# Gated delta: the 16x16 diagonal blocks inverted on VectorE by forward substitution, two doubling levels kept on TensorE

## The reference

```python
lower = jnp.where(strict, jnp.einsum('bhncd,bhned->bhnce', kb, k) * decay, 0.0)
tri = lower + jnp.eye(GDN_CHUNK, dtype=jnp.float32)
rhs = jnp.concatenate([v * beta[..., None], kb * jnp.exp(gc)[..., None]], axis=-1)
sol = lax.linalg.triangular_solve(tri, rhs, left_side=True, lower=True, unit_diagonal=True)
...
def step(state, xs):
    u_i, w_i, qh_i, kt_i, intra_i, gl_i = xs
    v_new = u_i - jnp.einsum('bhcd,bhde->bhce', w_i, state)
    o = (jnp.einsum('bhcd,bhde->bhce', qh_i, state)
         + jnp.einsum('bhce,bhef->bhcf', intra_i, v_new))
    state = (state * jnp.exp(gl_i)[..., None, None]
             + jnp.einsum('bhcd,bhce->bhde', kt_i, v_new))
    return state, o
```

## Time and profile before

| | us |
|---|---|
| median of 3 runs (2565.07 to 2569.24) | 2565.99 |
| span of the profiled execution | 2562.7 |
| PE busy (share of the span) | 2382.4 (93%) |
| DVE busy | 1392.5 (54%) |
| GpSimd busy | 1326.4 (52%) |
| ACT busy | 595.4 (23%) |

### The profile page before, as it was taken

How to read it: one execution, slowest core, us unless ns; L and a number is a source line. 1 busy time by engine, 2 the same in 40 slices (tenths; PEclk the granted TensorE clock), 3 DMA queues, 4 the chain that set the end, 5 groups by cost and what they waited for, 6 DMA issues and landing times.

```text
span 2562.7 us, 38766 instructions
## 1 busy us (share of the span) xinstructions
PE 2382.4 (93%) x14272; PEld 1896.6 (74%) x14272; DVE 1392.5 (54%) x1992; ACT 595.4 (23%) x1162; POOL 1326.4 (52%) x1018
## 2 busy tenths in 40 slices
PE   0888999998999999999999999999999999999996
PEld 0666777786777777777876877778777777887885
DVE  8965654656555554575135265155656554234536
ACT  0221210222323332232023022022322323224001
POOL 6673457434444445556655644644444444454763
PEclk9998999999999999999999999999999999999998
DMA  9864347322122123454325533532122222222542
GB/s 364 291 229 161 116 161 254 125 85 65 59 67 65 61 67 115 148 192 164 95 73 202 173 109 106 187 115 75 59 67 62 63 67 67 66 80 69 181 140 90
DMA packets 94600, 316.14 MB, mean 123 GB/s; under 512 B 10918, under 2 KB 11174, under 8 KB 93382
## 3 DMA queue, kind: packets, MB, share of 16 engines
q1 hardware_dynamic: 86768, 295.51, 34.1%
q10 hardware_dynamic: 7644, 18.16, 2.0%
HBM read 303.92 MB, written 8.39 MB: 122 GB/s over the span
## 4 chain that ended last, share of the span: by engine, by line
PE 71%; DVE 15%; POOLq 3%; ACT 3%; issue 3%; DMA 2%; POOL 2%; DVEq 1%; ACTq 1%; SPq 0%
PE bank L644 14%; PE bank L646 13%; PE bank L645 13%; DVE arena L1693 11%; PE bank L1159 4%; PE bank L1161 4%; PE bank L1160 4%; DVE acc L1693 3%; PE bank L925 2%; PE bank L954 2%; POOLq L1635 1%; POOL w_lo L1633 1%; ACT arena L1189 1%; PE bank L608 1%; PE bank L946 1%
## 5 line engine op out<-in xcount | busy, mean ns | idle before, releaser
L1629 POOL CAST w_hi<-ring 128x1024 fp32r<-128x1024 f32 (+1 forms) x320 | 363.5, 1136 | 1105.7 <-PE bank L646 922.6
L1633 POOL TENSOR_TENSOR w_lo<-ring,w_hi 128x512 fp32r<-128x512 f32 (+1 forms) x632 | 881.5, 1415 | 48.5 <-issue 1.3
L644 PE MATMUL bank<-h_hi,w_hi 128*128 128x512 f32 x1952 | 827.9, 424 | 14.1 <-POOLq L1635 12.3
L646 PE MATMUL bank<-h_hi,w_lo 128*128 128x512 f32 x1952 | 768.7, 394 | 0.0
L645 PE MATMUL bank<-h_lo,w_hi 128*128 128x512 f32 x1952 | 767.6, 393 | 0.0
L644 PEld LDWEIGHTS bank<-h_hi,w_hi 128*128 128x128 f32 x1952 | 370.6, 190 | 101.1 <-issue 16.4
L646 PEld LDWEIGHTS bank<-h_hi,w_lo 128*128 128x128 f32 x1952 | 369.1, 189 | 83.0
L645 PEld LDWEIGHTS bank<-h_lo,w_hi 128*128 128x128 f32 x1952 | 371.2, 190 | 69.3 <-issue 7.2
L1189 ACT ACTIVATE arena<-bank 128x512 f32<-128x512 f32 (+5 forms) x372 | 173.8, 467 | 737.5 <-PE bank L646 216.6
L1693 DVE SCALAR_TENSOR_TENSOR acc<-yT,cact,acc 128x1024 f32<-128x1024 f32 (+1 forms) x144 | 209.6, 1456 | 37.9 <-DMA acc<-in_b_mod 14.9
L1159 PE MATMUL bank<-w_hi,h_hi 128*128 128x512 f32 x448 | 175.4, 392 | 1.1 <-issue 1.1
(11 more groups left out here) (226 smaller groups left out, 2911.7 us busy)
## 6 DMA issues: line engine op xcount, KB each, us to landing
ring<-in_stream SPq DMA_DIRECT2D x352, 512.0 KB, 3.6
yT<-in_stream SPq DMA_DIRECT2D x128, 512.0 KB, 4.5
yT<-in_mod SPq DMA_DIRECT2D x32, 1024.0 KB, 8.2
arena<-in_x ACTq DMA_DIRECT2D x4, 1024.0 KB, 10.3
x_norm<-arena ACTq DMA_DIRECT2D x4, 1024.0 KB, 8.0
arena<-x_norm ACTq DMA_DIRECT2D x4, 1024.0 KB, 9.9
out<-arena SPq DMA_DIRECT2D x3, 1024.0 KB, 3.9
arena<-in_x SPq DMA_DIRECT2D x1, 2048.0 KB, 12.0
```

Of the source, the lines that this page charges most:

```text
L644: mm(PJ[b][:, :], hi, h_hi[:, k, :], start=(k == 0), stop=False)
L646: last = mm(PJ[b][:, :], lo, h_hi[:, k, :], start=False, stop=(k == KT - 1))
L1629: pool.tensor_copy(w_hi[:, par, 0:w], ring[:, slot, 0:w])
L1633: pool.tensor_tensor(w_lo[:, par, at], ring[:, slot, at], w_hi[:, par, at].bitcast(F32), ALU.subtract)
```

## The change

The first four diagonal levels are replaced. DVE masks `A(3)` to the strictly lower parts of the 16x16 diagonal blocks, and one reduction packs these into `base_l` (128 x 4 x 16). `base_x` starts as the identity, less the first column. For j = 1 to 14 a stream shuffle broadcasts row j of each 16-row block over its 16 partitions (`base_row`), a product with column j of `base_l` gives `base_part`, and a difference updates `base_x`; both have 4(j+1) elements per partition. One product with `base_at` spreads the result over `inv_n`. `LEVELS` is (16, 32), so three of five levels go from PE, DVE and ACT (and with them the first, 2x2, step of DVE). PE now makes the transpose: eight small matmuls in step 3 turn `inv_n`, and ACT copies the result to `invT_n`. The steps of a head go from 25 to 19, and the 64 k-steps are spread anew. DVE's and ACT's other work is put in a new order: `conv_k0` and `conv_k1` stand ahead of the copies to `inv_T`, `conv_q0`, `silu_k` and `conv_q1` behind the last of them, ACT's `tanh_k` in the second level and `tanh_q` behind `square_k`.

```diff
--- before.py
+++ after.py
-LEVELS = (2, 4, 8, 16, 32)
+BASE = 16
+LEVELS = (16, 32)
...
+        "base_lower": (row // BASE == col // BASE) & (col < row),
+        "base_eye": (row % BASE == col[:, :BASE]),
+        "base_at": (row % HALF_C // BASE == col[:, :HALF_C] // BASE),
...
-        gdn_fill = [5, 6, 5] + [2, 3, 2, 3, 2, 2, 2, 2, 3, 2, 2, 2, 2] + [2, 2, 2, 2, 3, 2, 2, 2, 2]
+        gdn_fill = [5, 7, 7] + [4, 3, 2, 3, 2, 3, 2] + [2, 3, 2, 3, 3, 3, 3, 3, 4]
...
                             if s == 3 + 2 * v:
 
-                                pe.wait_ge(S("gdn_ct"), D * 5 + v + 1)
-                                pe.wait_ge(S("gdn_T"), D * 10 + max(2 * v, 1))
+                                pe.wait_ge(S("gdn_ct"), D * len(LEVELS) + v + 1)
+                                pe.wait_ge(S("gdn_T"), D * 4 + v + 1)
+                                if v == 0:
+
+                                    for t in range(TT):
+                                        for rows, other in ((TOP, LOW), (LOW, TOP)):
+                                            mm(narrow(SB_[0])[other, t, :], inv_n[rows, t, :], ident[rows, rows],
+                                               start=True, stop=True)
...
+                                if v == 0:
+                                    fn(invT_n, narrow(SB_[0]), ACT.Copy)
                                 fn(lv_n[rows], narrow(TB[1])[rows], ACT.Copy).then_inc(S("gdn_lv"), 1)
-                                if v == 1:
+                                if v == 0:
                                     front(h, "square_q")
-                                if v >= N_LEVELS - 2 and not last:
-                                    front(h + 1, ("tanh_k", "tanh_q")[v - (N_LEVELS - 2)])
+                                if v == 1 and not last:
+                                    front(h + 1, "tanh_k")
...
                             if not last:
                                 front(h + 1, "square_k")
+                                front(h + 1, "tanh_q")
...
+                    ready("gdn_qk")
+                    tt(A(17), SB_[0][:, :], A(17), M).then_inc(S("gdn_intra"), 1)
+
+
+                    tt(tiles(A(14)), tiles(A(3)), over(C("base_lower").unsqueeze(1), BIG), M)
+                    reduce(base_l, A(14).rearrange("p (t b n) -> p t n b", t=TT, n=BASE), AX, Ad)
+                    cp(base_x, over(C("base_eye").unsqueeze(1), (P, TT, BASE)))
+                    tt(base_x[:, :, 0:1], base_x[:, :, 0:1], base_l[:, :, 0:1], Su)
+                    for j in range(1, BASE - 1):
+                        n = slice(0, j + 1)
+                        shuffle(base_row, base_x, [i // BASE * BASE + j for i in range(32)])
+                        tt(base_part[:, :, n], base_row[:, :, n], over(base_l[:, :, j:j + 1], (P, TT, j + 1)), M)
+                        tt(base_x[:, :, n], base_x[:, :, n], base_part[:, :, n], Su)
+                        if j == BASE // 2:
+                            ready("gdn_lT_copied")
+                            mask(0)
+                    blocks = (P, TT, HALF_C // BASE, BASE)
+                    tt(inv_n.rearrange("p t (b n) -> p t b n", n=BASE), over(base_x.unsqueeze(2), blocks),
+                       over(C("base_at").rearrange("p (b n) -> p b n", n=BASE).unsqueeze(1), blocks), M)
+                    sync().then_inc(S("gdn_T"), 1)
+
+                    mask(1)
+                    ready("gdn_vtanh")
+                    stt(A(10), A(5), 1.0, A(10), Ad, M).then_inc(S("gdn_v"), 1)
+                    ready("gdn_egb")
+                    tt(A(6), A(7), A(4), M).then_inc(S("gdn_qh"), 1)
+                    if not first:
+                        tail(h - 1)
+                    dve.wait_ge(S("gdn_TCT"), D * 4 + 1)
+                    tt(inv_n, inv_n, narrow(SB_[0]), Su).then_inc(S("gdn_T"), 1)
+                    tt(invT_n, invT_n, narrow(MB), Su).then_inc(S("gdn_T"), 1)
+                    ready("gdn_kT")
+                    tt(tiles(A(1)), tiles(TB[0][:, :]), per_token(4), M)
+                    tt(tiles(A(9)), tiles(TB[0][:, :]), per_token(5), M)
+                    dve.wait_ge(S("gdn_TCT"), D * 4 + 2)
+                    tt(inv_n, inv_n, narrow(SB_[0]), Su).then_inc(S("gdn_T"), 1)
+                    ready("gdn_vT")
+                    tt(tiles(A(8)), tiles(OB[:, :]), per_token(2), M)
+                    if not last:
+                        front(h + 1, "conv_k0")
+                        front(h + 1, "conv_k1")
+                    dve.wait_ge(S("gdn_TCT"), D * 4 + 3)
                     for half in range(2):
                         rows = (TOP, LOW)[half]
-                        dve.tensor_tensor(inv_n[rows], own(A(3), half),
-                                          over(C("merge1_c")[rows].unsqueeze(1), LOWER), M)
-                    sync()
-                    tt(inv_n, over(C("ident_c").unsqueeze(1), NARROW), inv_n, Su)
-                    ready("gdn_qk")
-                    tt(A(17), SB_[0][:, :], A(17), M).then_inc(S("gdn_intra"), 1)
-                    ready("gdn_lT_copied")
-                    mask(1).then_inc(S("gdn_ct"), 1)
-                    tt(masked[1], lT_swapped, over(C("mergeT1").unsqueeze(1), NARROW), M)
...
+                        dve.tensor_copy(own(inv_T, half), narrow(SB_[0])[rows])
+                    sync().then_inc(S("gdn_Tt"), 1)
+                    ready("gdn_ztanh")
+                    stt(A(19), A(18), 1.0, raw[:, 3, TAPS - 1:], Ad, M).then_inc(S("raw_used3"), 1)
+                    dve.wait_ge(S("gdn_TCT"), D * 4 + 4)
+                    ts(cross(inv_T), narrow(SB_[0])[TOP], -1.0, None, M).then_inc(S("gdn_Tt"), 1)
+                    if not last:
+                        front(h + 1, "conv_q0")
+                        front(h + 1, "silu_k")
+                        front(h + 1, "conv_q1")
                     for i in range(TT):
 
                         dve.wait_ge(S("rec_kv"), D * 4 + i + 1)
```

More of the change, by code:

```diff
@@ L378, in build @@
         inv_n, invT_n = narrow(A(11)), narrow(A(11)[:, NW:])
+        NB = TT * BASE
+        base_l, base_x, base_row, base_part = (
+            A(11)[:, NW + i * NB:NW + (i + 1) * NB].rearrange("p (t n) -> p t n", t=TT) for i in range(4))
         lT_n, lT_swapped = narrow(A(12)), narrow(A(12)[:, NW:])
@@ L1024, in delta @@
                         if s == REC - 3:
-                            pe.wait_ge(S("gdn_T"), D * 10 + 10)
+                            pe.wait_ge(S("gdn_T"), D * 4 + 4)
                             for t in range(TT):
@@ L2002, in mask @@
                     def mask(v):
-                        m = ((1,) + LEVELS)[v]
-                        return tt(masked[(v + 1) % 2], lT_n, over(C(f"mergeT{m}").unsqueeze(1), NARROW), M)
+                        return tt(masked[v % 2], lT_n, over(C(f"mergeT{LEVELS[v]}").unsqueeze(1), NARROW), M)\
+                            .then_inc(S("gdn_ct"), 1)
                     fill(state[:, :], 0.0)
@@ L2025, in delta @@
-                    sync().then_inc(S("gdn_T"), 1)
-                    for v in range(N_LEVELS):
-                        if v < len(LEVELS) - 1:
-                            mask(v + 2).then_inc(S("gdn_ct"), 1)
-                        if v == 0:
-                            ready("gdn_vtanh")
-                            stt(A(10), A(5), 1.0, A(10), Ad, M).then_inc(S("gdn_v"), 1)
-                            ready("gdn_egb")
-                            tt(A(6), A(7), A(4), M).then_inc(S("gdn_qh"), 1)
-                            if not first:
-                                tail(h - 1)
-                        if v == 1:
-                            ready("gdn_kT")
-                            tt(tiles(A(1)), tiles(TB[0][:, :]), per_token(4), M)
-                            tt(tiles(A(9)), tiles(TB[0][:, :]), per_token(5), M)
-                        if v == 2:
-                            ready("gdn_vT")
-                            tt(tiles(A(8)), tiles(OB[:, :]), per_token(2), M)
-                        if v == 4:
-                            ready("gdn_ztanh")
-                            stt(A(19), A(18), 1.0, raw[:, 3, TAPS - 1:], Ad, M).then_inc(S("raw_used3"), 1)
-                        if v == N_LEVELS - 1:
-                            dve.wait_ge(S("gdn_TCT"), D * 7 + N_LEVELS)
-                            for half in range(2):
-                                rows = (TOP, LOW)[half]
-                                dve.tensor_copy(own(inv_T, half), narrow(SB_[0])[rows])
-                            sync().then_inc(S("gdn_Tt"), 1)
-                        if not last:
-                            for part in ((), (), ("conv_k0",), ("conv_k1", "conv_q0"), ("conv_q1",), ("silu_k",))[v]:
-                                front(h + 1, part)
-                        dve.wait_ge(S("gdn_TCT"), D * 7 + v + 1 + v // (N_LEVELS - 1))
-                        if v < len(LEVELS) - 1:
-                            tt(inv_n, inv_n, narrow(SB_[0]), Su).then_inc(S("gdn_T"), 1)
```

(5 more changed lines are left out.)

16 lines of the change are left out of this document (7 added, 9 removed).

## The result

The changed kernel takes 2666.11 us (median; 2665.07 to 2672.59), the kernel before 2567.61 beside it: ratio 1.0388, 95% interval 1.0372 to 1.0404. It is slower, by 98.5 us. The profiled execution spans 2665.3 us, 102.6 more than the 2562.7 of before. First the page's busy times and its chain by engine, which answer to the earlier trace rows.

The account below looks back on a forecast made before the run. The kernel was taken as a stream of TensorE work, busy 93% of the span. Ten heads adding 89 us and two adding 7.5 brought the 2562.7 span to 2659, the median to 2662; forecast 2660, range 2585 to 2705.

Parts of the forecast that it names:

- TensorE's saving: Per head on PE: three levels -4.95, old waits -1.6, turning inv_n +0.4, together -6.2 us.
- The DVE chain: Mask, reduction, 14 rounds and building inv_n on DVE: ends 23.3 us after kk, PE ready at 16.5.
- Rival C: Substitution rounds on DVE are dearer (shuffle 0.42 us or costly short rows): 34 us more, 2695; chance 0.14.
- First wait: PE idle at step 3 for DVE's inv_n: 6.8 us a head, from 2.6 to about 10.
- The lock: DVE operations with two SBUF inputs wait for GpSimd's instruction under way: 2 us lost per split of weights.
- The second wait: PE idle at step 8, behind DVE's k convolution and ACT's queue: 4.6 us (0 to 5.5) in ten heads.
- The clock: PE's clock falls to 0.50 behind both waits: 2.0 us charged for one, 1.7 for the other.
- The sum: Ten heads +8.9 us each, 89 us; two last heads +3.75 each, 7.5 us; forecast 2660.
- A: Quiet DVE chain, GpSimd doesn't block small operations, clock stays up: waits 2.6 and 1.6, 2541 us; chance 0.12.
- B: Wait at step 3 as forecast, clock stays up, wait at step 8 only 1.6: 2592 us; chance 0.20.
- D: Waits and savings cancel over the kernel: 2566 us; chance 0.04.

Follow-up runs that it names:

- e11_retuned: Changed kernel with substitution scratch in PSUM, six more sets of projection products ahead of step 3, k convolution halves moved earlier; 2512.81 us, ratio 0.9799.
- e10_no_rounds_conv_early: Changed kernel without the 14 substitution rounds and with the next head's k convolution issued earlier on VectorE; 2522.09 us, ratio 0.9828.
- e1_psum: Changed kernel with the substitution's two scratch tiles in PSUM instead of SBUF; 2633.29 us, ratio 1.0265.
- e7_one_input_split: Changed kernel with GpSimd's two subtractions per weight split replaced by one-input copies; 2581.45 us, ratio 1.0067.
- e2_conv_early: Changed kernel with both halves of the next head's k convolution issued earlier on VectorE; 2614.65 us, ratio 1.0186.
- e9_no_rounds: Changed kernel with the 14 substitution rounds left out and the block reduction kept; 2567.06 us, ratio 0.9996.
- e5_filler: Changed kernel with 26 additional unread matmuls ahead of TensorE's wait of step 3 in every head; 2654.41 us, ratio 1.0353.
- e4b_both_fill7: Changed kernel with scratch in PSUM, earlier k convolution and seven more sets of projection products ahead of step 3; 2538.66 us, ratio 0.9883.

## Why the prediction was right

It gave 2660 (2585 to 2705), slower with 0.84; 2666 came. Point by point:

- **TensorE's saving, -6.2 us a head.** A head of `e11_retuned` less its wait is 61.1 us, against 67.05 before (the mean of four heads in DVE's timeline): -6.0. The step holds as a whole; its terms (4.95 for the levels, 1.6 for the old waits, 0.4 for the turn) were not measured one by one. `e10_no_rounds_conv_early` taken by its total would have misled me to -3.6; less its wait and its clock it gives -6.3.
- **The DVE chain.** It was laid out from `kk`: PE there at 16.5, six rounds done at 15.1, the end at 23.3. In the head shown PE is there at 16.48 (773.99 - 7.09 - 750.42), the sixth round ends at 15.17, and inv_n is built at 23.35. The forecast's 23.3 had the release in it, and PE starts at 23.57. The shuffle, for which no row of before existed, was taken at 0.23 us and is 0.23 at the median of 168; the reduction, taken at 1.23, is 1.06. Rival C (dearer rounds) falls by that row. First wait: 6.8 forecast, 7.1 in the head shown and 7.2 at the mean of ordinary heads. That it is 9.1 in the first head of each layer was not foreseen, which is 4 us in all.
- **The lock.** It carried the difference between a wait of 2.6 and one of 6.8, and was argued from two blocked copies. `e1_psum` shows it on the products. It was forecast at 4.2 us of the chain (23.3 - 19.1), with about 2 us lost at each split; in the head shown the first split costs 1.6 and the second 2.2. `e1_psum` took 3.3 off and left 0.6 in `mask(0)`, so 3.9, and the quiet wait comes to 3.4 where 2.6 was forecast. The rule that the Trainium skill gives (SBUF — State Buffer, section "SBUF: two separate sides"), an exclusive hold of the shared port pair against a Vector operation with two SBUF inputs, fits all three: products of 8 elements blocked, the same ones free with an operand in PSUM, and shuffles, which have one input, at 225 to 233 ns in all 168 cases. By the same rule it must be a GpSimd instruction that reads SBUF; the cast in `e7_one_input_split` is one, and blocked.
- **The second wait, 4.6.** It is 4.38, in ten heads, behind ACT's lv, with the tanh and the tile copy in front, as laid out; DVE's convolution under GpSimd's split is its source: the copy of 12 elements ahead of it took 0.84 us (183 ns for one of 24 in the earlier trace rows), its first operation 1.61 (0.49 in the earlier trace rows), and the next three 3.27 (1.57 for two in the earlier trace rows). That is 2.7 us lost where 3 were forecast, and leaves a quiet wait of 1.7 where 1.6 was forecast. `e7_one_input_split`, with shorter instructions on GpSimd, has 3.0. `e2_conv_early` removes the wait. `e9_no_rounds` shows that the substitution has no part in it. The prediction's step had it so (it counted the wait from the work behind vT alone), and I had lost sight of that in the theory of that run.
- **The clock, 3.7.** A head is 75.94; less 61.1, 7.2 and 4.4 that leaves 3.2. The granted clock gives the terms apart: 4.0 and 3.9 us of work at the low level in ordinary heads, 1.8 us for each by the rate of the matmuls, where 2.0 and 1.7 were charged. So both terms were about right for this kernel. `e5_filler` took the first away and gained only 1.1 a head, because the low stretch behind the second wait grew by 1.5 us. The term isn't a constant that goes with a wait: behind the same wait of 4.4 us it was 3.4 to 5.3 us of work here and up to 6.8 in `e9_no_rounds`. That the forecast chose near the right size is in part luck; its two rows of before had 3.2 and 4.1 us.
- **The sum.** +8.9 a head forecast; 75.94 - 67.05 is 8.9. Its terms are -6.0, +7.2, +4.4 and +3.2 instead of -6.2, +6.8, +4.6 and +3.7; the last of them is what is left over, and no check of the sum. That holds for an ordinary head. The ten heads that prepare another can be read as a whole, from the `kk` of a layer's first head to that of its last (layer 0, before and changed):

```profile
592.13:930.54 338.41, 328.14 (x2680) 260.81 (x2679) 199.57 (x300) 99.99 (x181) 153.35 (x121) 0.99 0.21 63
...
592.97:978.88 385.91, 323.99 (x2039) 264.20 (x2038) 236.34 (x535) 96.04 (x171) 148.65 (x121) 0.91 0.17 55
```

That is +47.5, and layer 1 has +49.8 (336.0 to 385.8): 97.3 us, where ten times 8.9 had been forecast. The excess lies in the first head of each layer, which takes 81.9 and 81.7 us instead of 70.2 and 68.4, +25 for the two where the forecast had 18: their waits are 9.1 us, with 5.4 us of work at the low clock behind, and 4.8 behind the second wait. Of the 102.6 us between the spans 5.3 are left, 0.8 of them ahead of the first head; the two last heads had been forecast at 7.5. So the sum missed by 6 us as +8 and -2, and why the last heads gave less stays open.
- **Rivals A, B and D.** A quiet chain (A) needed waits of 2.6 and 1.6 and no fall of the clock; the waits are 7.2 and 4.4, and the clock fell. B needed a clock that stays up and a quiet second wait of 1.6; the same rows refute both. D needed waits and savings that cancel; they add up to +8.9 a head.

## What to carry to other kernels

Work moved off the busiest engine pays only if the work that took its place is shorter than what the busy engine can do meanwhile: here 6 us a head were saved and 15 lost, and once the order was made anew, an ordinary head came down from 67.05 to 61.6 us, and the kernel by 53 us. When steps are removed, look also for what they covered: a transfer, a convolution or a queue that was never late before. A long chain of tiny operations on VectorE should have one operand of each in PSUM where GpSimd works on SBUF beside it.

## What the runs showed of the hardware

- A product and a difference of 8 elements together took 2.00 us beside GpSimd's subtractions and 0.40 with one operand in PSUM (754.98 to 755.38 in `e1_psum`); a GpSimd cast or copy with one input blocks them too, for its own shorter duration (pairs of 1.32 and 0.90 us instead of about 0.45).
- A shuffle of 128x64 takes 0.23 us (168 of them), also beside GpSimd's instructions, and loading its mask 0.01. A reduction of 128x512 with a stride takes 1.06 us to 64 results.
- A shorter wait is not always cheaper by as much: behind waits of 7.2 us 4.0 us of work ran at the granted clock of 0.50 (mean of ten heads), and behind waits of 4.65 us 6.0. In `e4b_both_fill7` the same wait of 2.74 us was followed by 3.4 us at the low level in seven heads and by none in the eighth. Keeping TensorE busy with 5.9 us of useless matmuls kept the clock at 1.00 behind the first wait and gained 1.1 us a head.
